# 22 more dummy products on TensorE ahead of V's first product in the opening of a two-layer GLA and pooling trunk

## The reference

```python
def run_layer(h, prompt, S0, buf, norm_g, w_in, ...):
    xn = rmsnorm(h, norm_g)
    z = xn @ w_in                     # (B, L, 6160): q k v ga u gb alow mg
    q, k, v, ga, u, gb, alow, mg = jnp.split(z, IN_OFFSETS, axis=-1)
    la = jax.nn.log_sigmoid(alow @ w_alpha + b_alpha) / GATE_TAU
    o, S_new = gla_scan(q, k, v, la, S0, chunk)      # gated linear attention
    y_pool = pool_mix(u, ...)                        # trailing means of u
    ya = (rms(o) * gain * silu(ga)) @ w_a
    yb = (y_pool * silu(gb)) @ w_b
    merged = sigmoid(mg_a) * ya + sigmoid(mg_b) * yb
    return h + merged @ w_out, S_new, buf_new
```

## Time and profile before

| what | us |
|---|---|
| median of 3 runs (1122.69, 1123.73, 1123.86) | 1123.73 |
| the profiled execution, own time | 1122.94 |
| its span, slowest core (5), first to last instruction | 1121.4 |
| spans of all eight cores | 1118.8 to 1121.4 |
| PE busy on core 5 | 1092.8 (97%) |
| mean granted TensorE clock, all cores | 0.993 to 0.995 |

### The profile page before, as it was taken

One profiled execution on the slowest core, in us unless ns is written; L12 is line 12 of the kernel. 1 busy time (PEld: TensorE's weight loads), 2 busy tenths in 40 slices (PEclk: granted clock), 3 DMA queues, 4 the chain that ended last, 5 costly groups with the idle time before them and its releaser, 6 DMA issues.

```text
span 1121.4 us, 27773 instructions; the slowest of 8 cores (1118.8 to 1121.4 us)
## 1 busy us (share of the span) xinstructions
PE 1092.8 (97%) x9958; PEld 856.6 (76%) x9958; DVE 673.9 (60%) x1087; ACT 515.0 (46%) x1052; POOL 601.6 (54%) x925
## 2 busy tenths in 40 slices
PE   7999999999999999999989999999999999999996
PEld 3687777786887777778757877787788867787785
DVE  5368767655845765565554776656666376656554
ACT  2646565665432434234237465655544323433333
POOL 5178788876853433343343787787776323333332
PEclk8999999999999999999999999999999999999998
DMA  9964666674596989898687234444545966845521
GB/s 196 198 132 124 140 120 134 150 156 91 102 178 153 276 264 291 222 270 229 163 142 189 53 86 92 75 88 101 110 74 135 195 210 202 270 157 188 203 68 58
DMA packets 123210, 176.20 MB, mean 157 GB/s; under 512 B 82384, under 2 KB 89040, under 8 KB 118976
## 3 DMA queue, kind: packets, MB, share of 16 engines
q1 hardware_dynamic: 107808, 138.38, 42.3%
q0 software_dynamic: 15264, 36.05, 22.0%
HBM read 138.55 MB, written 53.01 MB: 171 GB/s over the span
## 4 chain that ended last, share of the span: by engine, by line
PE 90%; DMA 3%; issue 2%; POOL 2%; DVE 1%; ACT 1%; POOLq 0%; DVEq 0%; ACTq 0%
PE psum L562 90%; DMA arena<-w 2%; ACT arena L589 1%; POOL arena L604 1%; DVE arena L616 1%; DVE arena L604 0%; POOL arena L611 0%; DMA arena<-hin 0%; PE psum L568 0%; POOL arena L623 0%; POOL arena L636 0%; DVE arena L611 0%; POOLq L246 0%; DVEq L269 0%; DVE arena L623 0%
## 5 line engine op out<-in xcount | busy, mean ns | idle before, releaser
L562 PE MATMUL psum<-arena 128*128 128x256 bf16 (+6 forms) x9854 | 1088.7, 279 | 22.4 <-DVE arena L604 4.9
L562 PEld LDWEIGHTS psum<-arena 128*128 128x128 bf16 (+2 forms) x9854 | 850.4, 98 | 256.0 <-issue 19.6
L604 POOL TENSOR_TENSOR arena<-arena 128x256 bf16<-128x256 f32 (+12 forms) x345 | 340.4, 991 | 299.7 <-DVE arena L616 233.2
L616 DVE SCALAR_TENSOR_TENSOR arena<-arena,psum 128x256 f32<-128x256 f32 (+7 forms) x472 | 265.6, 600 | 186.8 <-PE psum L562 142.7
L589 ACT ACTIVATE arena<-psum,arena 128x256 f32<-128x256 f32 (+3 forms) x432 | 173.3, 456 | 306.0 <-PE psum L562 253.0
L589 ACT ACTIVATE arena<-psum 128x256 bf16<-128x256 f32 (+7 forms) x258 | 159.0, 630 | 183.2 <-PE psum L562 162.5
L611 POOL TENSOR_SCALAR arena<-arena 128x256 f32<-128x256 f32 (+7 forms) x378 | 169.5, 457 | 103.6 <-ACT arena L589 57.6
L589 ACT ACTIVATE arena<-arena 128x1024 bf16<-128x1024 f32 (+4 forms) x144 | 141.5, 996 | 94.4 <-DVE arena L616 50.7
L616 DVE SCALAR_TENSOR_TENSOR arena<-psum,arena 128x512 f32<-128x512 f32 (+6 forms) x195 | 125.2, 656 | 62.0 <-PE psum L562 50.9
L616 DVE SCALAR_TENSOR_TENSOR arena<-arena 128x256 bf16<-128x256 f32 (+4 forms) x124 | 112.8, 919 | 63.7 <-POOL arena L604 59.2
L636 POOL DMA_DIRECT2D arena<-w x106 | 62.3, 590 | 49.4 <-PE psum L562 32.1
(11 more groups left out here) (10 smaller groups left out, 21.3 us busy)
## 6 DMA issues: line engine op xcount, KB each, us to landing
arena<-hin SPq DMA_DIRECT2D x32, 512.0 KB, 6.9
arena<-sgla SPq DMA_DIRECT2D x16, 1024.0 KB, 8.5
nsg_s<-arena SPq DMA_DIRECT2D x16, 1024.0 KB, 6.8
arena<-w POOLq DMA_DIRECT2D x30, 512.0 KB, 14.9
arena<-w POOLq DMA_DIRECT2D x48, 224.0 KB, 5.0
arena<-XN SPq DMA_DIRECT2D x20, 512.0 KB, 5.9
H<-arena SPq DMA_DIRECT2D x16, 512.0 KB, 4.8
arena<-H SPq DMA_DIRECT2D x16, 512.0 KB, 5.0
```

What stands on the lines that cost most here:

```text
L562: return S.add("pe", lambda e: e.matmul(out, lhsT=lhsT, rhs=rhs, start=start, stop=stop, skip_group_check=sgc), r=[lhsT, rhs] + list(also_ ...
L604: return S.add(eng, lambda e: e.tensor_tensor(out=out, in0=in0, in1=in1, op=op), r=[in0, in1], w=[out], after=after, cost=c)
L616: return S.add("dve", lambda e: e.scalar_tensor_tensor(out=out, in0=in0, scalar=scalar, in1=in1, op0=op0, op1=op1), r=r, w=[out], cost=eco ...
```

## The change

`mm` can name operations that must come first (`after`), and `warm` can add `more` dummies, of the same shape and in the same bank as its last ones, which come after the last PE operation listed so far. `front` asks for 22 of them with tile 2, where that last operation is the last of tile 1's transposes. For the planner each costs 100 ns.

```diff
-        def mm(out, lhsT, rhs, start, stop, sgc=False, share=1.0, also_r=(), also_w=()):
+        def mm(out, lhsT, rhs, start, stop, sgc=False, share=1.0, also_r=(), also_w=(), after=()):
...
-                         r=[lhsT, rhs] + list(also_r), w=[out] + list(also_w), cost=c, lat=250.0, attach=True)
+                         r=[lhsT, rhs] + list(also_r), w=[out] + list(also_w), after=after, cost=c, lat=250.0, attach=True)
...
-        def warm(n, cold=False):
+        def warm(n, cold=False, more=0, after=()):
...
+            for i in range(more):
+                k = mm(bank(b_), ones[:, 0:128], ones, True, True, after=after)
+                S.ops[k]["cost"] = 100.0
             banks.free(b_)
...
-                        warm((20, 9, 9, 8)[t], t == 0)
+                        warm((20, 9, 9, 8)[t], t == 0, (0, 0, 22, 0)[t], [S.last_of("pe")] if t else ())
```

## The result

| | kernel before | changed kernel |
|---|---|---|
| median, us (22 runs each, in turns) | 1124.04 | 1126.26 |
| profiled execution, us | 1122.94 | 1126.36 |
| slowest core's span, us | 1121.4 | 1124.8 |
| ratio of the runs, 95% interval | | 1.0016 [1.0009, 1.0022] |

The changed kernel is slower, by 0.16% or 1.8 us. In some executions the cores of one die get a mean clock of 0.81 to 0.98 and take longer (three of the changed kernel's 22, at 1293 to 1327 us): the medians include these, while the ratios, their intervals and the means over runs further down leave them out. The forecast was a gain of 0.4 us and a time of 1123.3 us with a range up to 1124.8; 1126.3 lies above it. The difference is just inside the 0.2% that the prediction called "the same", and its interval excludes no difference.

What follows compares the result with a forecast made beforehand. PE, busy 97%, was taken as the bound, slowed by a low clock in the opening. Of 2.2 us gained there, weights and an earlier load leave 0.4 on the slowest core: 1123.3 us, range 1121.5 to 1124.8.

Steps and rivals of the forecast that it cites:

- The dummies' time: Gap before V's first product: 22 dummies take 4.7 us and end at 19.55, making V 0.2 us late on core 5.
- The clock: Opening, through V: granted clock stays at 1.00, so tile 3's transposes come at 22.45 instead of 24.67, gaining 2.2 us.
- The weights take the gain: From 8 to 72 us: full DMA engines make PE wait for weights, some 1.5 to 2.2 us on cores without slack.
- the slack of 1.4 us: Core 5 near transfer 13: weights land 1.4 to 1.5 us before use, so that much of 2.2 is kept.
- a time of its own, which PE doesn't set: Weights' stream, 8 to 72 us: its timing is independent of PE, so an earlier PE only waits.
- spool: SP's load at 53.6 us: issued up to 2 us sooner, it delays U by up to 0.6 us; 0.3 taken.
- The sum by core: Spans over the cores: core 5 1120.3, core 0 1120.4, slowest core 6 at 1121.0 to 1121.1, a gain of 0.4 us.
- Every wait is relative, so what is left is carried to the end: Behind 63 us: DMA engines are free, so the gain remaining there reaches the kernel's end unchanged.
- No DMA or other engine is touched: Dummies in the gap: only PE writes their bank and nobody reads it, so there is no cost beyond their own time.
- The whole gain (1): Whole kernel: all 2.2 us from the opening's clock arrive, time 1121.5; chance 0.12.
- The fall of the clock one step later (2): Opening, PE idle between 22 and 24.5 us: clock falls there, V's work runs at half speed, 1124.9 us; chance 0.10.
- The fall among the dummies (3): Gap, at 17.9 us: dummies don't hold the clock, V starts 2 us late and slow, 1125.7 us; chance 0.04.

Runs made afterwards that it cites:

- e9: Kernel before, moving only 16 columns each of weight transfers 5 and 6 (Q, layer 0), the rest zeroed by POOL; gap unfilled: 1123.76 us, ratio 1.0000.
- e10: e3's kernel (gap filled, count kept) with the same lightened weight transfers as e9: 1121.14 us, ratio 0.9971 to the kernel before.
- e1: Kernel before with 22 products of 32 columns more at the program's start, none in the gap: 1127.39 us, ratio 1.0014.
- e5: Kernel before with 26 long dummies of tiles 1 to 3 replaced by 154 of 80 columns, 128 products more, gap unfilled: 1124.66 us, ratio 1.0002.
- e6: Kernel before with 6 products of 32 columns more at the program's start, gap unfilled: ratio 1.0007.
- e3: Changed kernel with 22 small products fewer at the program's start, so PE's count is as before: 1125.07 us, ratio 0.9994; repeated 1125.20 us, 1.0003.
- e2: Changed kernel with 110 dummies of 80 columns in the gap and 23 short for five long ones, 128 products over the kernel before: 1126.43 us, ratio 1.0003.
- e7: Changed kernel with 88 dummies of 124 columns in the gap in place of 22 of 512: ratio 1.0019 to the kernel before.
- e4: Changed kernel with 64 dummies of 172 columns in the gap in place of 22 of 512: ratio 1.0008 to the kernel before.

## Why the prediction missed

- **The dummies' time: right.** 22 were to end at 19.55; V's first product begins at about 19.56, as 23 start from 14.81 on at 0.214 us each (19.78, the transposes, less 0.214). It is 0.2 us late on core 5, as worked out.
- **The clock: right.** At 1.00 from 15 to 26 us on all cores. Tile 3's transposes were forecast at 22.45 and came at 22.44, pair 1's alpha products near 24.5 and came at 24.45; in the mean of the cores these transposes come 1.9 us sooner (24.1 and 22.3). The penalty rule of the Trainium skill ("TensorE: Matmul & The Clock Gate", section Terms) would have given 3.4 us; the trace agrees with the lower number, as the idle part of the low stretch was no loss.
- **The weights take the gain: right in kind.** New waits of 1.5 to 2.2 us on cores with no slack were forecast; the mean of all cores is 1.9. e9 and e10 show it: without that limit the gain reaches the end.
- **Where and how much: a missed term.** The failed step is the slack of 1.4 us that the sum lets core 5 keep: it kept none, and its key transposes, forecast at 70.3 to 71 us, came at 72.87. I read the slack at transfer 13 only. On core 5 the waits come at transfers 6 to 8, between 37 and 47 us; four other cores wait at 62 to 64 us too. And the stream, which I took to have "a time of its own, which PE doesn't set", got later: in the mean of the cores transfer 8 landed at 43.8 and lands at 45.4, transfer 13 at 62.2 and 62.9. I had looked for loads that move forward, and named only `spool`. That one didn't move (53.6 and 54.7 us on core 5, means 53.1 and 53.4). Three others did, 2.2 us sooner on core 5, 1.7 to 1.9 in the mean; before, then after:

```profile
28.74 0.35 SPq L636 DMA_DIRECT2D arena<-gfull  x1
35.07 0.97 SPq L636 DMA_DIRECT2D arena<-hin  x2
```

```profile
26.48 0.35 SPq L636 DMA_DIRECT2D arena<-gfull  x1
32.82 0.92 SPq L636 DMA_DIRECT2D arena<-hin  x2
```

  They are 512 KB each, beside a stream that fills the DMA engines. By the prediction's own working for `spool` (2.2 of some 10 us, 113 KB, at 150 KB per us) each may put up to 0.75 us ahead of the weights, enough for the 1.6 us. This cause is argued, not shown: transfer 8's mean landing also differs between kernels that don't fill the gap (43.8 in the kernel before, 44.3 to 45.0 in e1, e5 and e6), and no run held these loads back. The profile of the kernel before is the most favourable of them. Over the four profiles without the gap filled transfer 8 lands at 44.4 us and the waits for weights are 0.9; over the eight with it, light weights left out, 45.1 and 1.9. So some 0.7 us of the 1.6 go with the gap, the rest with the execution that I read. By this term the slowest core keeps nothing, where 0.4 us were forecast; e3's two ratios, 0.9994 and 1.0003, agree with either.
- **The sum by core: luck at best.** It takes each core's span and slack from one execution and finds the slowest in core 6, by 0.1 to 0.4 us. In 85 timed runs of the kernel before, one core's span scatters with a standard deviation of 1.0 to 1.7 us, and every core is the slowest in some: core 6 in 17, core 5 in 11, core 3 in 3. A gain of 0.4 us can't be worked out that way.
- **"Every wait is relative, so what is left is carried to the end": wrong, and it made the sign.** The instruction fetches don't go with the rest. In the mean of the cores the difference was 0.6 us at 650 us, and 2.0 at the end; the 1.4 between are made in two places, behind transposes that take 1 to 1.7 us longer. e1 has this loss without the gap's dummies, e3 has the dummies without the loss, and with a full packet of instructions more (e2 and e5) it is gone. With -0.7 to 0.3 us for the gap (e3's two ratios) and 1.6 to 1.7 for the count, the sum is 0.9 to 2.0 us slower; the ratio says 1.8.
- **"No DMA or other engine is touched": wrong in the same way.** 44 instructions more are a DMA matter. The row was on the page of before as well (78 packets of q8), and I costed it at nothing without a word.
- **The rivals.** The whole gain (1) didn't come. The fall of the clock one step later (2) is there on core 6, at 0.62 from 25 to 29 us, with the mechanism as told; PE waited for weights behind it on that core too (1.1 us), and core 6 is not the slowest there, so it didn't set the time of that execution. The fall among the dummies (3) didn't occur in the changed kernel, but it did on three cores of e3 and two of its repetition. None of the three had the price of a count, and the 0.04 left for the unseen was too little.
- **What stays open.** Which of the hit transposes cost PE time (e7's loss). No run moved one fetch alone, so that the fetch makes the transpose late rests on the order of the packets. The step at 842 us has the longer transpose at 833 behind it, but it was seen only in kernels with 22 products more and not tried by itself. The slowest core lost 3.4 us in the profiled executions, where the mean of the cores lost 2.0: of the 1.4 between, 0.9 is there from 50 us on, as core 5 got its weights later than the rest, and I have no cause for the spread.

## What to carry to other kernels

In this kernel products added to PE's stream, even free ones in an idle gap, moved the fetches of what follows, by as many products in the median. So when a kernel has DMA transposes that just meet their readers, add or remove instructions with the total kept (drop as many elsewhere), or try one more variant with another count, before a result of 0.1 to 0.2% is put down to the edit itself. A slack that is under the scatter of one core's span between executions needs several of them. And where an opening is bound by a full DMA stream, look for every load that is issued behind the work that gets faster, and find the slack at each transfer, not at one.

## What the runs showed of the hardware

- A DMA transpose of this kernel that no other data DMA and no fetch of PE's overlaps takes 3.05 us (59 of them in the two traces, 3.02 to 3.25). With a fetch of PE's instructions between its issue and its landing (23 of them) the median is 4.7 us, the longest 5.04, and 3.04 where the fetch comes just behind the last packets. All but one of the 23 are those at 642 us and, in the changed kernel, at 1066; the latter have packets of the other instruction queue in them too. At 642 us one packet of 16.4 KB ahead of the transpose's last two makes it 1.7 us longer.
- A wait of PE can cost more than its idle time. On core 0 of e4 the granted clock falls to 0.50 at 129.4 us, for 3.4 us, behind a wait of 3.01; on core 7 of e6 at 871.9 behind one of 2.04. By the clock such a stretch costs up to 1.7 us more. Behind 1.74 us on core 3 of e6, and behind the 1.1 us at 129.3 us of core 0 in the kernel before, it stayed at 1.00.
- In e3's profile cores 6 and 7 have the granted clock at 0.81 for some 5 us at a time, near 38, 61, 121, 166, 420 and 435 us. The profiles of before and after show none of this; those of e1, e2, e4 and e3's repetition have from one to three such stretches, on cores 4 to 7 alone.
- PE's instructions come 256 to a packet of 16.4 KB. Two to a product this gives 77.8 packets before, 78.0 in the changed kernel, 78.3 in e4, 78.5 in e7 and 78.8 in e2 and e5, and the pages have 78, 78, 79, 79 and 79. 256 instructions more cost nothing that could be measured (1.0002 and 1.0003).
- The order of all engines but PE was the same in both kernels, and so was PE's but for the 22. The orders show no difference behind 20 us, while the times differ at 660.
